# PEER experts in a transformer block: all experts for all tokens, or one indirect gather per chosen slot

## The chip, the cores and the metric

The kernel runs on one core of a Trainium2 chip. The metric is the device time of one execution in microseconds (us); the kernel before was timed three times.

## The reference, cut to what matters

One block of a trunk model for 512 latent tokens of width 2048 (`x1` is the residual after the mixer and the first layer norm). Everything ahead of the PEER layer is left alone by the change except the way its result is handed over. PEER has 8 heads. Each head picks for each token 16 of 16,384 experts, and an expert is one row `u` and one row `v` of 2048 fp32 numbers:

```python
s1, i1 = lax.top_k(s[..., 0, :], PEER_TOPK)
s2, i2 = lax.top_k(s[..., 1, :], PEER_TOPK)
cand_s = (s1[..., :, None] + s2[..., None, :]).reshape(B_, T, PEER_HEADS, n_cand)
cand_i = (i1[..., :, None] * PEER_N_KEYS + i2[..., None, :]).reshape(B_, T, PEER_HEADS, n_cand)
top_s, pos = lax.top_k(cand_s, PEER_TOPK)
idx = jnp.take_along_axis(cand_i, pos, axis=-1)
gates = jax.nn.softmax(top_s, axis=-1).astype(h.dtype)
...
act = jax.nn.gelu(jnp.einsum('nkd,nd->nk', u[i_blk], h_blk), approximate=False)
return jnp.einsum('nk,nkd->nd', g_blk * act, v[i_blk])
```

So each token has 8 x 16 = 128 chosen pairs of rows. The output is `layer_norm(ALPHA * x1 + gate2 * peer, ln2_g, ln2_b)`.

## The kernel before

The stages run one behind the other; a barrier of all engines stands between two of them. `modulation`, `in_projection`, `rglru` and `rwkv` are not touched. `out_projection` ends in a layer norm with channels on the partitions: its result `x1` goes to DRAM, and `h2` is kept split in two fp32r halves, `h_hi` and `h_lo` ([128, 16, 512], channel tiles by tokens). `queries` projects `h2` and takes the 16 best keys of each half head (`best_key`, `best_val`).

`route` takes the tokens in four tiles of 128. Per tile VectorE (DVE) adds the pairs of scores, finds the 16 best of 256 for 8 heads, looks their key numbers up and makes the softmax. Then it builds one-hot matrices (`hot1`, `hot2`, L1685), GpSimd (POOL) puts the gates on one of them (L1581), TensorE (PE) multiplies them (L1603), and so a dense array of gates, 128 x 128 experts by 512 tokens, comes to DRAM as `gates_scratch` (32 MB).

`experts` then computes every expert for every token, in 16 groups of 8 chunks of 128 experts. A unit is 1 MB of weights: SP loads it (`raw`), ScalarE (ACT) copies it to fp32r (`hi`, L1738), DVE makes the rest (`lo`, L1752), and PE multiplies in three passes (hi x hi, hi x lo, lo x hi; L1798), 48 matmuls of 128x512 per unit. A group has 8 `u` units, whose results go through Gelu and are weighted with the gates (loaded by POOL, L1728), and 8 `v` units, whose results DVE adds to `f` (L1769). There are 256 units, 128 of `u` and 128 of `v`. `final` scales, adds `x1`, takes the second layer norm and stores the output. Two buffers each hold `raw`, `hi` and `lo`.

Of the kernel before, what the change touches and what calls it, by code (L numbers as in the profile page):

```python
# [163 lines left out]

# [156 lines left out]

# [143 lines left out]

# [145 lines left out]

# [3 lines left out]

# [54 lines left out]

# [367 lines left out]

# [97 lines left out]

# [48 lines left out]

# [86 lines left out]

# [117 lines left out]

def out_projection(nc, e, a):

    with ExitStack() as ctx:
# [14 lines left out]

        def finish(ctx, sb, normed):
            h2 = [sb(f"h2{b}", [P, LAT]) for b in range(2)]  # L1440
            modded, hi_done, lo_done, stored = sems(nc, ctx, "h2_modded", "h2_hi_done", "h2_lo_done", "x1_stored")

            def on_dve(dve, k):

                dve.wait_ge(normed, k + 1)
                nc.vector.tensor_scalar(h2[k % 2][:], z[:, k, :], e.one_plus_scale2[:, k:k + 1], e.mod[:, 3 * KT + k, 0:1], ALU.mult, ALU.add
                                        ).then_inc(modded, 1)
                dve.wait_ge(hi_done, k + 1)
                nc.vector.tensor_tensor(e.h_lo[:, k, :], h2[k % 2][:], e.h_hi[:, k, :].bitcast(FP32), ALU.subtract).then_inc(lo_done, 1)

            def on_act(act):
                for k in range(KT):
                    act.wait_ge(modded, k + 1)
                    nc.scalar.activation(e.h_hi[:, k, :], h2[k % 2][:], ACT.Copy).then_inc(hi_done, 1)

            def on_sp(sp):
                for q in range(4):
                    sp.wait_ge(normed, 4 * q + 4)
                    sp.dma_start(e.x1_dram[:, 4 * q:4 * q + 4, :], z[:, 4 * q:4 * q + 4, :]).then_inc(stored, 16)
                sp.wait_ge(stored, 64)  # L1460

            return on_act, on_dve, on_sp
# [9 lines left out]

# [15 lines left out]

# [42 lines left out]

R_STEPS = 16
SPREAD = 4
DEPTH = 4
BANKFUL = 4

def route(nc, e, a):

    with ExitStack() as ctx:
        sb = lambda n, s, d=FP32: ctx.enter_context(nc.sbuf_tensor("rt_" + n, s, d))
# [16 lines left out]
        tiles, turns, fills = LAT // P, P // SPREAD, P // BANKFUL
        per_turn = SPREAD // BANKFUL  # L1560
        with nc.Block() as block:
            @block.sync
            def _(sp):
                for dst, src in ((ident, a["ident"]), (iota, a["iota"])):
                    sp.dma_start(dst[:], src).then_inc(const_loaded, 16)
                sp.sem_inc(dense_free, 1)

                with sp.Fori(0, tiles) as t:
                    sp.wait_ge(bank_read, (t + 1) * fills + 4)
                    sp.dma_start(e.gates_dram[:, :, bass.ds(t * P, P)], dense[:]).then_inc(stored, 16)  # L1570
                    sp.wait_ge(stored, 16 * t + 16)
                    sp.sem_inc(dense_free, 1)
# [12 lines left out]
            def _(pe):
                pe.sem_inc(hot_used, DEPTH * per_turn)
                pe.sem_inc(turned, 1)
                pe.wait_ge(const_loaded, 32)
                with pe.Fori(0, tiles) as t:
                    pe.wait_ge(chosen_ready, t + 2)  # L1590
                    pe.wait_ge(sel_ready, t + 1)
                    for j in range(3):
                        last = nc.tensor.transpose(t_acc[:, j * P:(j + 1) * P], chosen[:, j, :], ident[:])
                    last.then_inc(turned, 1)
                    with pe.Fori(0, turns // DEPTH) as i:
                        for b in range(DEPTH):
                            turn = t * turns + DEPTH * i + b
                            pe.wait_ge(gated_ready, turn + 1)
                            for n in range(SPREAD):
                                f = n // BANKFUL  # L1600
                                if n % BANKFUL == 0:
                                    pe.wait_ge(bank_read, turn * per_turn + f + 1)
                                ins = nc.tensor.matmul(g_acc[(b * per_turn + f) % 4][:, (n % BANKFUL) * NK:(n % BANKFUL + 1) * NK],  # L1603
                                                       hot1[b][:, n, :], gated[b][:, n, :], start=True, stop=True)
                                if n % BANKFUL == BANKFUL - 1:
                                    ins.then_inc(hot_used, 1)

            @block.scalar
            def _(act):
                act.sem_inc(sel_ready, 1)  # L1610
                act.sem_inc(bank_read, 4)
                with act.Fori(0, tiles) as t:
                    act.wait_ge(shifted, t + 1)
                    nc.scalar.activation(chosen[:, 2, :], top[:].rearrange("p h k -> p (h k)"), ACT.Exp).then_inc(exp_done, 1)
# [384 lines left out]
```

## Time and profile before

| | us |
|---|---|
| three runs, median (lowest to highest) | 6884.99 (6883.69 to 6888.27) |
| the profiled execution, first to last instruction (its span) | 6879.0 |
| the profiled execution's own time | the record holds its span alone; the median of the runs lies 6.0 above the span |
| PE busy in the span | 6061.1 (88%) |
| DVE busy | 2778.5 (40%) |
| ACT busy | 1685.7 (25%) |
| POOL busy | 366.5 (5%) |
| moved by DMA, all told | 595.47 MB, mean 87 GB/s |

A busy engine is one that executes an instruction; several can be busy at once, so the shares don't add up to one. The PE clock column of a window is the granted clock as a share of 2.4 GHz: 1.00 is 2.4 GHz and 0.50 is 1.2 GHz. The DMA share is the mean busy share of the core's 16 DMA engines.

### The profile page before, as it was taken

How to read it: one execution, taken by the hardware profiler on the slowest of the kernel's cores; microseconds unless marked ns; L12 is line 12 of the kernel's file. 1: busy time of each engine (PE TensorE's matmuls, PEld its weight loads, DVE VectorE, ACT ScalarE, POOL GpSimd, SP SyncE). 2: the span in 40 equal slices, each digit the busy share in tenths (PEclk: the TensorE clock that was granted, in tenths of full speed). 3: DMA queues.
4: the chain of work that ended last, by engine and by line, in shares of the span. 5: the costliest groups of instructions: out<-in, count | busy, mean ns of one | idle time of the engine just before them, and what ended most of it. 6: DMA issues, size and time to landing. Idle time of an engine off the chain costs nothing. (4 is left out here: it accounts for less than half of the span.)

```text
span 6879.0 us, 80488 instructions
## 1 busy us (share of the span) xinstructions
PE 6061.1 (88%) x32312; PEld 4951.1 (72%) x32312; DVE 2778.5 (40%) x3717; ACT 1685.7 (25%) x1951; POOL 366.5 (5%) x426
## 2 busy tenths in 40 slices
PE   6798988699999999959664569999999999999997
PEld 1687855687788877837453458888888888888885
DVE  1333433443433444232579933333333333333333
ACT  0111225333332333222213312222222222222222
POOL 0000010000000000010003400000000000000000
PEclk8899999788887888769887789999999999999998
DMA  5222275100000000031204353333333333333332
GB/s 227 91 86 82 102 250 182 41 21 11 11 8 8 21 11 11 1 109 61 98 31 79 67 144 110 110 106 107 110 110 110 105 108 108 110 110 106 107 108 86
DMA packets 199453, 595.47 MB, mean 87 GB/s; under 512 B 16884, under 2 KB 121972, under 8 KB 146292
## 3 DMA queue, kind: packets, MB, share of 16 engines
q1 hardware_dynamic: 176160, 477.24, 21.2%
q0 software_dynamic: 22976, 115.63, 5.0%
q8 instruction: 135, 2.21, 0.1%
q14 instruction: 34, 0.28, 0.0%
q10 hardware_dynamic: 148, 0.10, 0.0%
HBM read 531.84 MB, written 61.09 MB: 86 GB/s over the span
## 5 line engine op out<-in xcount | busy, mean ns | idle before, releaser
L1798 PE MATMUL ex_u<-h_hi,ex_hi 128*128 128x512 f32 x2048 | 797.6, 389 | 52.5 <-DVE ex_lo L1752 52.5
L1798 PE MATMUL ex_u<-h_lo,ex_hi 128*128 128x512 f32 x2048 | 797.4, 389 | 0.0
L1798 PE MATMUL ex_u<-h_hi,ex_lo 128*128 128x512 f32 x2048 | 797.3, 389 | 0.0
L1798 PE MATMUL ex_v<-ex_w_hi,ex_hi 128*128 128x512 f32 x2048 | 796.7, 389 | 0.0
L1798 PE MATMUL ex_v<-ex_w_lo,ex_hi 128*128 128x512 f32 x2048 | 796.7, 389 | 0.0
L1798 PE MATMUL ex_v<-ex_w_hi,ex_lo 128*128 128x512 f32 x2048 | 796.7, 389 | 0.0
L1738 ACT ACTIVATE ex_hi<-ex_raw 128x2048 fp32r<-128x2048 f32 x256 | 490.3, 1915 | 1100.8 <-PE ex_v L1798 1100.3
L1752 DVE TENSOR_TENSOR ex_lo<-ex_raw,ex_hi 128x2048 fp32r<-128x2048 f32 x256 | 586.5, 2291 | 84.1 <-ACT ex_hi L1738 84.1
L1769 DVE TENSOR_TENSOR f<-f,ex_v 128x512 f32<-128x512 f32 x256 | 164.5, 684 | 843.1 <-PE ex_v L1798 843.1
L1798 PEld LDWEIGHTS ex_u<-h_hi,ex_hi 128*128 128x128 f32 x2048 | 384.9, 188 | 132.7 <-DVE ex_lo L1752 52.7
L1759 DVE TENSOR_TENSOR ex_w<-ex_act,ex_gates 128x512 f32<-128x512 f32 x128 | 88.7, 693 | 882.2 <-ACT ex_act L1743 882.2
L1798 PEld LDWEIGHTS ex_u<-h_hi,ex_lo 128*128 128x128 f32 x2048 | 384.8, 188 | 80.0
L1798 PEld LDWEIGHTS ex_u<-h_lo,ex_hi 128*128 128x128 f32 x2048 | 384.8, 188 | 79.8
L1798 PEld LDWEIGHTS ex_v<-ex_w_hi,ex_lo 128*128 128x128 f32 x2048 | 384.4, 188 | 79.9
L1798 PEld LDWEIGHTS ex_v<-ex_w_lo,ex_hi 128*128 128x128 f32 x2048 | 384.4, 188 | 79.8
L1798 PEld LDWEIGHTS ex_v<-ex_w_hi,ex_hi 128*128 128x128 f32 x2048 | 384.4, 188 | 79.7
L1743 ACT ACTIVATE ex_act<-ex_u 128x512 f32<-128x512 f32 x128 | 76.8, 600 | 1077.3 <-PE ex_u L1798 1077.3
L994 DVE TENSOR_TENSOR rw_X<-rw_bank,rw_level_mask 128x512 f32<-128x512 f32 x240 | 164.4, 691 | 398.3 <-PE rw_bank L1110 396.9
L250 PE MATMUL pb_acc<-x_hi,pb_hi 128*128 128x512 f32 x832 | 213.0, 338 | 72.8 <-DVE pb_lo L221 72.8
L1685 DVE TENSOR_TENSOR rt_hot<-rt_iota,rt_sel 128x512 f32<-128x512 f32 x256 | 259.1, 1088 | 7.8 <-ACT rt_sel L1617 7.8
L1603 PE MATMUL rt_g<-rt_gated,rt_hot 128*128 128x128 f32 x1024 | 186.1, 339 | 86.2 <-POOL rt_gated L1581 85.2
L605 PE MATMUL late_acc<-lru_late_w,cond_act 128*1 128x128 f32 x2048 | 229.2, 275 | 28.1 <-DMA lru_late_w<-in_ada_late 28.1
(349 smaller groups left out, 9245.2 us busy)
## 6 DMA issues: line engine op xcount, KB each, us to landing
ex_raw<-in_peer_u SPq DMA_DIRECT2D x128, 1024.0 KB, 4.8
ex_raw<-in_peer_v SPq DMA_DIRECT2D x128, 1024.0 KB, 4.8
lru_late_w<-in_ada_late POOLq DMA_DIRECT2D x64, 1024.0 KB, 5.1
ada_w<-in_ada_w SPq DMA_DIRECT2D x8, 4096.0 KB, 20.8
gates_scratch<-rt_dense SPq DMA_DIRECT2D x4, 8192.0 KB, 38.9
ex_gates<-gates_scratch POOLq DMA_DIRECT2D x128, 256.0 KB, 3.0
pb_raw<-in_w_in SPq DMA_DIRECT2D x26, 1024.0 KB, 4.8
pl_raw<-in_w_in SPq DMA_DIRECT2D x18, 1024.0 KB, 4.8
```

Source lines behind the costliest of these rows:

```text
L250: last = nc.tensor.matmul(acc[b][s][:], wt[b][:, ks], x[:, k, c0:c0 + w], start=(k == 0 and n == 0), stop=(k == KT - 1 and n == 2))
L605: last = nc.tensor.matmul(late_acc[rows % 2][part:part + 1, col:col + P], e.cond_act[:, k, 0:1], late_w[n % LATE_BUFS][:, k * P:(k + 1) * ...
L994: nc.vector.tensor_tensor((X if level > 1 else T)[:, 4 * q:4 * q + 4, :], take(("X", level, q))[:].rearrange("p (h n) -> p h n", h=4), mas ...
L1603: ins = nc.tensor.matmul(g_acc[(b * per_turn + f) % 4][:, (n % BANKFUL) * NK:(n % BANKFUL + 1) * NK], hot1[b][:, n, :], gated[b][:, n, :], ...
L1685: ins = nc.vector.tensor_tensor(dst[:], iota[:, None, :].to_broadcast(full), sel[:, m, at, None].to_broadcast(full), ALU.is_equal)
L1738: nc.scalar.activation(hi[u % 2][:], raw[u % 2][:], ACT.Copy).then_inc(hi_done, 1)
L1743: nc.scalar.activation(act_[c % 2][:], u_acc[c % 2][:], ACT.Gelu).then_inc(gelu_done, 1)
L1752: nc.vector.tensor_tensor(lo[u % 2][:], raw[u % 2][:], hi[u % 2][:].bitcast(FP32), ALU.subtract).then_inc(lo_done, 1)
L1759: nc.vector.tensor_tensor(w[c % 2][:], act_[c % 2][:], gates[c % 2][:], ALU.mult).then_inc(weighted, 1)
L1769: nc.vector.tensor_tensor(t, t, v_acc[v % 2][h][:], ALU.add).then_inc(added, 1)
L1798: ins = nc.tensor.matmul(out, wt, x, start=first and n == 0, stop=last and n == 2)
```

## The change

`route`, the old `experts` and `final` go. The host lays `u` and `v` side by side, so that `peer_uv` has 16,384 rows of 16 KB. `out_projection` keeps `h2` in fp32, and a new stage, `token_major`, transposes `x1` and `h2` with 128 PE transposes so that tokens lie on the partitions; `x1` goes to DRAM in that layout.

The new `experts` takes the four token tiles and, in each, 128 slots (8 heads x 16). A slot is one indirect gather by POOL: for each of 128 tokens the row of its expert, 128 x 16 KB = 2 MB, into one of five buffers `uv`. DVE makes the dot product of the `u` half with `h2` (`dot`, written over the `u` half), ACT the Gelu of one column, DVE a diagonal matrix of gelu times gate (`weigh`), and PE four fp32 matmuls of 128x512 that add diagonal times `v` into four PSUM banks of `f_acc`. The choice of experts (`route`) is now cut in ten parts. The first tile's are all made ahead of the slots; those of the next tile stand between slots 6, 14, ... 78 of the tile before. `finish` (the residual and the second layer norm, token-major) of a tile stands at slots 3 and 4 of the next one.

```diff
-        e.gates_dram = nc.dram_tensor("gates_scratch", [NK, NK, LAT], FP32, kind="Internal").ap()
+        token_major(nc, e, a, z, h2)
...
+        fills = [(src, q, t) for src in range(2) for q in range(4) for t in range(TOK_TILES)]
...
+                sp.wait_ge(act_taken, 2 * TOK_TILES)
+                sp.wait_ge(dve_taken, 2 * TOK_TILES)
+                sp.dma_start(e.x1_dram.rearrange("t p d -> p t d"), x1_tok[:]).then_inc(stored, 16)
+                sp.wait_ge(stored, 16)
...
+                    for j in range(4):
+                        ins = nc.tensor.transpose(banks[n % 8][:, j * P:(j + 1) * P],
+                                                  (x1, h2)[src][:, 4 * q + j, t * P:(t + 1) * P], ident[:])
...
+                        nc.scalar.activation(dst[src][:, t, q * BANK:(q + 1) * BANK], banks[n % 8][:], ACT.Copy).then_inc(act_taken, 1)
...
+                        nc.vector.tensor_copy(dst[src][:, t, q * BANK:(q + 1) * BANK], banks[n % 8][:]).then_inc(dve_taken, 1)
...
+ROUTE_PARTS = 10
+ROUTE_AT = 6
+ROUTE_EVERY = 8
+FINAL_AT = 3
+SLOTS = PEER_HEADS * TOPK
+BUFS = 5
+DIAGS = 4
...
+            def _(pool):
+                for n in range(total_slots):
+                    t, s = n // SLOTS, n % SLOTS
+                    if s == 0:
+                        pool.wait_ge(chosen_ready, t + 1)
+                    if n >= BUFS:
+                        pool.wait_ge(slot_used, n - BUFS + 1)
+                    pool.indirect_dma_start(uv[n % BUFS][:], None, a["peer_uv"],
+                                            bass.IndirectOffsetOnAxis(expert[:, t, s:s + 1], 0)).then_inc(uv_loaded[n % BUFS], 16)
...
+                    pe.wait_ge(diag_ready, n + 1)
+                    for c in range(D // BANK):
+                        ins = nc.tensor.matmul(f_acc[t % 2][:, c * BANK:(c + 1) * BANK], diag[n % DIAGS][:],
+                                               uv[n % BUFS][:, D + c * BANK:D + (c + 1) * BANK], start=s == 0, stop=s == SLOTS - 1)
+                    ins.then_inc(slot_used, 1)
...
+                def root(t):
+                    act.wait_ge(var_ready, t + 1)
+                    nc.scalar.activation(rstd[:], mv[:, 1:2], ACT.Ln, bias=eps[:]).then_inc(ln_done, 1)
+                    act.wait_ge(ln_done, t + 1)
+                    nc.scalar.activation(rstd[:], rstd[:], ACT.Exp, scale=-0.5).then_inc(rstd_ready, 1)
...
+                    act.wait_ge(dotted, n + 1)
+                    nc.scalar.activation(gelu[:, t, s:s + 1], dots[:, t, s:s + 1], ACT.Gelu).then_inc(gelu_done, 1)
...
+                def dot(n):
+                    t, s, b = n // SLOTS, n % SLOTS, n % BUFS
+                    dve.wait_ge(uv_loaded[b], 16 * (n // BUFS + 1))
+                    nc.vector.tensor_tensor_reduce(out=uv[b][:, 0:D], in0=uv[b][:, 0:D], in1=e.h2_tok[:, t, :], op0=ALU.mult, op1=ALU.add,
+                                                   scale=1.0, scalar=0.0, accum_out=dots[:, t, s:s + 1]).then_inc(dotted, 1)
+
+                def weigh(n):
+                    t, s = n // SLOTS, n % SLOTS
+                    dve.wait_ge(gelu_done, n + 1)
+                    if n >= DIAGS:
+                        dve.wait_ge(slot_used, n - DIAGS + 1)
+                    nc.vector.tensor_scalar(diag[n % DIAGS][:], ident[:], gelu[:, t, s:s + 1], gate[:, t, s:s + 1], ALU.mult, ALU.mult
+                                            ).then_inc(diag_ready, 1)
...
+                for n in range(total_slots):
+                    t, s = n // SLOTS, n % SLOTS
+                    dot(n)
+                    if n:
+                        weigh(n - 1)
+                    if t and s in (FINAL_AT, FINAL_AT + 1):
+                        finish(t - 1, s - FINAL_AT)
+                    part, off = divmod(s - ROUTE_AT, ROUTE_EVERY)
+                    if t + 1 < TOK_TILES and off == 0 and 0 <= part < ROUTE_PARTS:
+                        route(t + 1, part)
...
+    a["peer_uv"] = np.concatenate([g["peer_u"][0], g["peer_v"][0]], axis=1)
```

What DVE has in a row in the `experts` stage of before, inside a group's `u` units (`ex_w_hi`, `ex_w_lo` are the weighted activations in two halves; line numbers are those of the kernel before):

```order
L1752 TENSOR_TENSOR ex_lo0<-ex_raw0,ex_hi0 128x2048
L1757 REGISTER_ALU
L1759 TENSOR_TENSOR ex_w1<-ex_act1,ex_gates1 128x512
L1760 REGISTER_ALU
L1761 CAST ex_w_hi<-ex_w1 128x512
L1763 TENSOR_TENSOR ex_w_lo<-ex_w1,ex_w_hi 128x512
```

What DVE has there in the changed kernel, around slot 3 of the second tile (line numbers of the changed kernel; the first `ISA` row is the dot product, the second writes its sum out):

```order
L1653 ISA ex_uv1,ex_dots<-ex_uv1,h2_tok 128x2048
L1653 ISA ex_dots 128x1
L1661 TENSOR_SCALAR ex_diag2<-ex_ident,ex_gelu,ex_gate 128x128
L1671 TENSOR_TENSOR ex_z<-ex_f0,ex_rows 128x2048
L1673 SCALAR_TENSOR_TENSOR ex_z<-ex_x1,ex_z 128x2048
L1677 BN_STATS ex_stats<-ex_z 128x6 x4
L1679 BN_AGGR ex_mv<-ex_stats 128x2
L1653 ISA ex_uv2,ex_dots<-ex_uv2,h2_tok 128x2048
L1653 ISA ex_dots 128x1
```

One subtraction of 128x2048 per MB of weights has become one product with a sum per 2 MB gathered, and the diagonal follows it one slot late; pieces of `finish` and `route` stand in the same queue.

What PE has from the end of `route` into `experts` before (`rt_g` is the dense array's bank; the loops' bookkeeping stands between), where each unit is 48 matmuls, 12,288 in all:

```order
L1603 MATMUL rt_g3<-rt_gated3,rt_hot1_3 128x128 x4
L1595 REGISTER_ALU
L1595 COMPARE_AND_BRANCH
L1589 REGISTER_ALU
L1589 COMPARE_AND_BRANCH
L1561 UNCONDITIONAL_BRANCH
L1791 UNCONDITIONAL_BRANCH
L1801 UNCONDITIONAL_BRANCH
L1801 ISA
L1798 MATMUL ex_u0<-h_hi,ex_hi0 128x512
L1798 MATMUL ex_u0<-h_lo,ex_hi0 128x512
L1798 MATMUL ex_u0<-h_hi,ex_lo0 128x512
```

And in the changed kernel, one row per slot, 512 rows:

```order
L1576 MATMUL ex_f0<-ex_uv0,ex_diag0 128x512 x4
L1576 MATMUL ex_f0<-ex_uv1,ex_diag1 128x512 x4
L1576 MATMUL ex_f0<-ex_uv2,ex_diag2 128x512 x4
L1576 MATMUL ex_f0<-ex_uv3,ex_diag3 128x512 x4
L1576 MATMUL ex_f0<-ex_uv4,ex_diag0 128x512 x4
```

The 12,288 fp32r matmuls have become 2,048 fp32 matmuls, each group of four waiting for its diagonal.

## Rows read from the trace of the kernel before

**Rows 1.** Windows by stage: start:end, length, busy (instructions) of each engine, PE clock, DMA share, GB/s.

```profile
0.00:3322.00 3322.00, 2857.27 (x18028) 2310.36 (x18028) 1230.41 (x1508) 890.22 (x1331) 129.99 (x170) 0.85 0.20 70
3322.00:3546.00 224.00, 195.84 (x896) 160.22 (x896) 139.97 (x657) 38.61 (x32) 0.00 (x0) 0.93 0.23 80
3546.00:4003.00 457.00, 189.68 (x1036) 161.49 (x1036) 391.54 (x591) 138.17 (x136) 166.22 (x128) 0.69 0.36 74
4003.00:6804.00 2801.00, 2787.40 (x12288) 2307.57 (x12288) 979.78 (x897) 594.82 (x416) 70.25 (x128) 1.00 0.32 108
6804.00:6879.00 75.00, 30.93 (x64) 11.47 (x64) 36.80 (x66) 23.89 (x36) 0.00 (x0) 0.75 0.30 113
```

**Rows 2.** The page's costliest groups, experts and route stages.

```profile
L1798 PE MATMUL ex_u<-h_hi,ex_hi 128*128 128x512 f32 x2048 | 797.6, 389 | 52.5 <-DVE ex_lo L1752 52.5
L1738 ACT ACTIVATE ex_hi<-ex_raw 128x2048 fp32r<-128x2048 f32 x256 | 490.3, 1915 | 1100.8 <-PE ex_v L1798 1100.3
L1752 DVE TENSOR_TENSOR ex_lo<-ex_raw,ex_hi 128x2048 fp32r<-128x2048 f32 x256 | 586.5, 2291 | 84.1 <-ACT ex_hi L1738 84.1
L1685 DVE TENSOR_TENSOR rt_hot<-rt_iota,rt_sel 128x512 f32<-128x512 f32 x256 | 259.1, 1088 | 7.8 <-ACT rt_sel L1617 7.8
```

**Rows 3.** Groups of instructions by line.

```profile
L900 DVE TENSOR_TENSOR_SCAN rw_cum<-rw_restart,rw_sg 128x1024 f32<-128x1024 f32 x12 | 27.4, 2282 | 2.5 <-ACT rw_sg L825 2.5
L1728 POOL DMA_DIRECT2D ex_gates<-gates_scratch x128 | 70.2, 549 | 2664.7 <-DVE ex_w L1759 2608.3 <-DVEq L1748 43.3 <-issue 13.0
L857 ACT ACTIVATE rw_T<-rw_bank 128x512 f32<-128x512 f32 x240 | 143.3, 597 | 379.8 <-PE rw_bank L1123 379.8
```

**Rows 4.** Timeline of PE, transposes in rwkv.

```profile
1271.04 1.94 PE L1075 MATMUL rw_bank<-rw_ident,rw_Bt 128*128 128x128 f32 x8 [11.90 <-DVEq L942]
```

**Rows 5.** Timeline of the first route tile: start, length, instruction, [idle before it].

```profile
3550.89 2.29 DVE L1648 TENSOR_TENSOR rt_score<-best_val 128x2048 f32 x1 [2.54 <-DMA rt_iota<-in_iota]
3569.89 0.31 ACT L1614 ACTIVATE rt_chosen<-rt_top 128x128 f32<-128x128 f32 x1 [37.59 <-DVE rt_top L1658]
3584.44 0.29 DVE L1672 TENSOR_TENSOR rt_chosen<-rt_chosen,rt_total 128x128 f32<-128x128 f32 x1
```

**Rows 6.** Windows of three stretches with loaded DMA engines (columns as in rows 1).

```profile
14.00:70.00 56.00, 55.94 (x138) 12.33 (x139) 0.33 (x2) 1.76 (x3) 0.00 (x0) 1.00 1.01 434
910.00:920.00 10.00, 7.40 (x66) 5.34 (x63) 9.90 (x11) 0.00 (x0) 1.62 (x3) 0.93 1.03 413
3018.00:3030.00 12.00, 0.00 (x0) 0.00 (x0) 3.70 (x3) 3.82 (x2) 9.87 (x9) 0.50 1.04 387
```

**Rows 7.** DMA issues: out<-in, queue, count, KB each, median us from issue to landing.

```profile
ex_raw<-in_peer_u SPq DMA_DIRECT2D x128, 1024.0 KB, 4.8
gates_scratch<-rt_dense SPq DMA_DIRECT2D x4, 8192.0 KB, 38.9
out_dram<-f SPq DMA_DIRECT2D x4, 1024.0 KB, 4.3
```

**Rows 8.** Timeline of PE's weight loads in the first matmuls on `ada_w`.

```profile
16.57 0.13 PEld L142 LDWEIGHTS ada_acc<-ada_w,cond_act 128*2 128x2 f32 x1 [0.72 <-issue]
17.42 0.13 PEld L142 LDWEIGHTS ada_acc<-ada_w,cond_act 128*2 128x2 f32 x1 [0.72 <-issue]
18.79 0.09 PEld L142 LDWEIGHTS ada_acc<-ada_w,cond_act 128*2 128x2 f32 x1 [0.34 <-issue]
19.22 0.09 PEld L142 LDWEIGHTS ada_acc<-ada_w,cond_act 128*2 128x2 f32 x1 [0.34 <-issue]
```

**Rows 9.** Window of a route stretch (columns as in rows 1).

```profile
3596.00:3656.00 60.00, 40.05 (x232) 34.09 (x230) 58.00 (x58) 30.99 (x30) 36.34 (x28) 0.86 0.00 0
```

**Rows 10.** Groups of DVE instructions in the first route tile.

```profile
L1486 DVE MATCH_REPLACE8 rt_rest<-rt_top,rt_score 128x256 f32<-128x256 f32 x8 | 3.2, 436 | 0.0
L1483 DVE FIND_INDEX8 rt_pos<-rt_top,rt_score 128x8 uint32<-128x256 f32 x8 | 3.2, 427 | 0.0
```

**Rows 11.** Groups of instructions in the last 79 us.

```profile
L1392 ACT ACT_TABLE_LOAD x1 | 1.3, 1283 | 0.0
```

More of the change, by code:

```diff
@@ L1453, in on_act @@
                     act.wait_ge(modded, k + 1)
[L1454 to L1462, printed above, removed]
-        layer_norm(nc, a, "ln1_", z, a["ln1_g"], a["ln1_b"], finish)
+                    nc.scalar.activation(e.h_hi[:, k, :], h2[:, k, :], ACT.Copy).then_inc(hi_done, 1)
@@ L1559, in route @@
[L1559 to L1560 removed]
+        expert_f = sb("expert_f", [P, P])
+        expert, gate = sb("expert", [P, TOK_TILES, SLOTS], U32), sb("gate", [P, TOK_TILES, SLOTS])
+        dots, gelu = sb("dots", [P, TOK_TILES, SLOTS]), sb("gelu", [P, TOK_TILES, SLOTS])
+        uv = [sb(f"uv{b}", [P, 2 * D]) for b in range(BUFS)]
+        diag = [sb(f"diag{b}", [P, P]) for b in range(DIAGS)]
+        rows = sb("rows", [P, 3, D])
@@ L1584, in _ @@
             @block.tensor
             def _(pe):
[L1586 to L1606, printed above, removed]
@@ new lines, in _ @@
+                for part in range(ROUTE_PARTS):
+                    route(0, part)
+                for n in range(total_slots):
+                    t, s = n // SLOTS, n % SLOTS
+                    dot(n)
[6 more added lines that the diff above has]
+                        route(t + 1, part)
@@ new lines, in _, with best_part @@
+                weigh(total_slots - 1)
+                finish(TOK_TILES - 1, 0)
+                finish(TOK_TILES - 1, 1)
+EXP_PART = 4
+def best_part(nc, c, landed, vals, positions, source, other, n, part):
+    at = slice(8, 16) if part == 2 else slice(0, 8)
+    src = other if part == 2 else source
+    if part in (0, 2):
+        nc.vector.tensor_copy(landed[:, 0:1], landed[:, 1:2])
+        for r in range(n):
+            ins = nc.vector.max(vals[:, r, at], src[:, r, :])
+        c.ordered(ins)
+    if part in (1, 2):
+        nc.vector.tensor_copy(landed[:, 0:1], landed[:, 1:2])
+        for r in range(n):
+            ins = nc.vector.max_index(positions[:, r, at], vals[:, r, at], src[:, r, :])
+        if part == 1:
+            for r in range(n):
+                ins = nc.vector.match_replace(other[:, r, :], vals[:, r, at], src[:, r, :], LOWEST)
+        c.ordered(ins)
@@ L1884, in tail @@
             out_projection(nc, e, a)
-            with ExitStack() as picks:
-                e.best_key, e.best_val = (picks.enter_context(nc.sbuf_tensor(n, [P, TOK_TILES, HP, TOPK], FP32))
-                                          for n in ("best_key", "best_val"))
-                queries(nc, e, a)
-                route(nc, e, a)
-            f = inner.enter_context(nc.sbuf_tensor("f", [P, KT, LAT], FP32))
-            experts(nc, e, a, f)
-            final(nc, e, a, f, out)
+            queries(nc, e, a)
+        experts(nc, e, a, out)
 def position_tables():
```

403 lines of the change are left out of this document (153 added, 250 removed).

## Prediction, written before the run

> **What bounds the kernel now.** I read the windows by stage first. The last three stages, which the change replaces, take 3333 us of the 6879: 457 for `route`, 2801 for `experts`, 75 for `final` [rows 1]. In `experts` PE is busy for 2787 of 2801 us at clock 1.00, while the DMA engines are busy for 0.32 of it. So the stage is as long as PE's 12,288 matmuls: 2801 / 12,288 = 0.228 us each. The groups of the page agree: a matmul waits for nothing but the first unit (52.5 us over all groups), and ACT stands idle for 1100 us until PE frees a buffer [rows 2]. In `route` DVE is busy for 392 of 457 us [rows 1]. Everything ahead of 3546 us stays, but for one stage put in.
>
> **The change, part by part.** *Removed:* all that lies behind 3546, 3333 us.
>
> *`token_major`, added ahead of the queries.* 128 transposes of 128x128. The trace has eight such in 1.94 us, with PE just out of an idle stretch of 11.9 us [rows 4], so 0.24 each or 31 us for all; once PE runs at its higher clock, half, 16. ACT and DVE take 16 fills each: at 0.60 us (the eviction of 128x512 in [rows 3]) that is 10 us beside it. The 4 MB store of `x1` starts after half of the fills, 8 to 15 us, and at the best rate below (434 GB/s) moves for 10 us and lands some 2 later. I take 26 us with the barrier, from 20 to 40.
>
> *Head of the stage.* Choosing the first tile's experts is DVE's old chain: from 3546 the first sum starts at 3550.89 and the softmax ends at 3584.7 [rows 5]; two small operations of 0.3 come on top: 39 us, nothing beside it. Then a first gather must land: 1 MB takes 4.8 us from issue to landing [rows 7], of which 1.05 MB / 434 GB/s = 2.4 is moving, so 2.4 is latency; with POOL's issue 3 us beyond the transfer itself.
>
> *The 512 slots.* Four resources serve a slot, and the slowest sets its length.
> - DMA: 128 x 16,384 B = 2.097 MB, 1074 MB for all slots. The stretch 14 to 70 us, where loads of `ada_w` (rows of 32 KB) queue behind each other, shows all 16 engines full (share 1.01) at 434 GB/s; two other full stretches, with shorter rows mixed in, give 413 and 387 [rows 6]. That is 4.83, 5.08 and 5.42 us a slot. Rows of 16 KB lie between, scattered reads may cost something: I take 5.1.
> - PE: four fp32 matmuls of 128x512. Each has two weight loads in the trace, and these follow each other every 0.85 us at first and every 0.43 us afterwards [rows 8]; the clock over the stretch is 1.00 in the mean [rows 6], so these are the two levels, 1.2 and 2.4 GHz. A matmul is then 0.86 us at 2.4 GHz, a slot 3.4; at 1.2 GHz 6.8.
> - DVE: the dot product reads 2 x 2048 numbers as `ex_lo` does, 2.29 us [rows 2], then a sum is written out and a 128x128 diagonal made, 0.15 + 0.3: 2.75. The product with a running sum is not in the trace. The other bound is the scan, which also carries a sum: 1024 elements in 2.28 us [rows 3], so 4.5 for 2048, and 4.95 a slot. I take the former, since a sum over the row needs no result per element. The Trainium skill ("Vector Engine (DVE) Microarchitecture Reference", section 7, Points that are easy to get wrong) says that a scalar-tensor-tensor shape with two sources in SBUF that aren't bf16 halves its throughput, since no port is left to read the accumulator back; by it the slot would be DVE's 4.95 too, and no run here has shown it.
> - POOL: one issue. A plain DMA of 128 rows is 0.55 us [rows 3]; an indirect one reads 128 indices as well. Above I bound it by an operation of DVE that it may have to wait out, 0.55 + 2.29 = 2.8. Both lie under 5.1.
>
> So the slot is the DMA engines' 5.1 us: 512 x 5.1 = 2611 us. That holds while enough gathers are queued. A buffer comes round every 5 x 5.1 = 25.5 us. From landing to `slot_used` it needs the dot (2.3), the next slot's landing and dot (5.1, since `weigh` stands one slot late), 0.3 and PE's 3.4: 11.4 with waits. Issue, latency and its own transfer are 0.6 + 2.4 + 5.1 = 8.1. The remaining 6 us are the slack.
>
> *Stalls.* DVE's long pieces eat into that slack. The longest part of `route` is 8 x (0.427 + 0.436) and small loads, some 8 us [rows 10]; the others are at most two operations of 2.29. `finish` is about 7 us at slot 3, and at slot 4 a wait for ACT with two table loads of 1.28 [rows 11], then 6: 16 together. Per tile (16 - 6) + (8 - 6) = 12 at most, less what DVE regains in the 2.35 us that each slot leaves it; 20 us for three tiles.
>
> *Tail.* Behind the last landing: dot 2.3, Gelu and diagonal 0.6, PE 3.4, `finish` 7 + 3 + 6, and 1 MB out in 4.3 [rows 7], 28 us with waits.
>
> *Sum:* 3546 + 26 + 39 + 3 + 2611 + 20 + 28 = 6273 against the span of 6879. The median of the runs is 6885, 6 above the span, so I say 6279. Slots of 4.83 to 5.42 us make it 6140 to 6440.
>
> 2. *Scattered rows come slower, but above the break-even.* The loads of 1 MB in `experts` show 108 GB/s at share 0.32 [rows 1], 338 GB/s if that share were 1. At 338 to 390 a slot is 5.4 to 6.2 us, 6430 to 6840. 13%, with the case of the rule in it.
> 3. *Slower than before: the gather falls under the break-even.* The stage may cost 3333 - 26 - 39 - 3 - 28 = 3237 us, so 6.32 us a slot, 332 GB/s. The place is the read side, 128 scattered addresses per gather. The price, with 300 GB/s, is 7.0 us a slot and 7250. For it: the only far row of a worse pattern, the 8 MB store of short pieces in 38.9 us [rows 7], runs at 216 GB/s. Against it: its pieces are 512 B, and these are 16 KB. 10%.
> 4. *PE stays at 1.2 GHz,* because it rests between slots: 6.8 us a slot, and then 7150. Against it: at the lower level PE would work without a rest, and in `route` PE at 0.67 busy was granted 0.86 [rows 9], which makes 4.0 us a slot, under 5.1. It decides from a mean clock of 0.67. 4%.
> 5. *POOL's indices cost over 6.3 us.* Nothing in the trace prices that. 3%.
> 6. *Ties* within 0.2%, which is about what a measurement of this kernel can tell from no change: 2%.
>
> **How the numbers follow.** The forecast (DMA-bound, 4.8 to 5.42 us) has 58%; rivals 1 to 6 have 10, 13, 10, 4, 3 and 2. Faster by over 0.2%: 58 + 10 + 13 = 81%; within 0.2%: 2%; slower: 17%. The range reaches from 6120, just under 4.83 us a slot, to 6760, a slot of 6.05, which takes in rival 1 and most of rival 2; about 2 in 10 stay outside, nearly all above.
>
> **What the profile after would show.** Right: DMA share near 1 and 400 to 440 GB/s between about 3620 and 6240; `ex_uv` landing in a steady beat of 5.1; DVE's dot released by the DMA of `ex_uv`; PE idle for a third of the time and released by the diagonal; POOL released by PE's `slot_used`. Wrong in the price of the dot: its row would say 4.4 us in place of 2.3. Wrong in the clock: matmuls of a slot in 6.8 us and the DMA share at 0.75. Wrong in POOL: the issue row long and POOL never idle. Rivals 2 and 3: DMA share near 1, but fewer GB/s. The forecast fails most easily by the rate of scattered rows, since each 0.1 us of a slot is 51 us.

## The result, and the profile after

The changed kernel takes 6201.74 us, the median of 4 runs (6191.05 to 6207.8), against 6886.63 before (4 runs, 6883.69 to 6897.67). The ratio is 0.9001, 95% interval 0.8989 to 0.9014. The profiled execution took 6191.05 us, with a span of 6189.4. Faster was forecast, at 6279 us: 77 above the measurement, inside the range.

The windows by stage, with the columns of [rows 1]: what stays, `token_major`, the queries, the head of the new stage, its slots, its tail.

```profile
0.00:3322.00 3322.00, 2857.73 (x18028) 2311.31 (x18028) 1226.72 (x1503) 888.12 (x1329) 130.62 (x170) 0.85 0.20 69
3322.00:3348.00 26.00, 16.73 (x128) 16.49 (x128) 14.24 (x22) 10.81 (x18) 0.00 (x0) 0.75 0.29 119
3348.00:3572.00 224.00, 196.24 (x896) 160.51 (x896) 136.45 (x634) 38.59 (x32) 0.00 (x0) 0.94 0.24 85
3572.00:3620.00 48.00, 0.00 (x0) 0.00 (x0) 37.31 (x111) 1.59 (x2) 4.30 (x5) 0.50 0.34 118
3620.00:6160.00 2540.00, 1917.79 (x4080) 752.07 (x4080) 1446.38 (x1818) 125.31 (x535) 709.43 (x508) 0.98 1.00 425
6160.00:6189.40 29.40, 7.13 (x16) 2.96 (x16) 14.52 (x14) 3.27 (x5) 0.00 (x0) 0.69 0.08 36
```

Where 3333 us were replaced, 2643 now stand: 26 of `token_major` and 2617 from 3572 on. The resource that is full has changed: in [rows 1] PE was busy all through `experts` and the DMA engines for 0.32; from 3620 to 6160 us it is the DMA engines, share 1.00 at 425 GB/s in the mean, and PE is busy for 0.76. The groups of instructions from 3560 us on say the same by what ended each engine's idle time:

```profile
L1576 PE MATMUL ex_f<-ex_uv,ex_diag 128*128 128x512 f32 x4096 | 1924.9, 615 | 680.0 <-DVE ex_diag L1661 679.6
L1653 DVE CUSTOM_DVE_ANT_0 ex_uv<-ex_uv,h_tok 128x2048 f32<-128x2048 f32 x512 | 1173.5, 2292 | 1098.0 <-DMA ex_uv<-in_peer_uv,ex_expert 1097.3
...
L1565 POOL DMA_INDIRECT ex_uv<-in_peer_uv,ex_expert x512 | 713.7, 1394 | 2384.1 <-PE ex_f L1576 1797.5 <-DVE ex_expert L1647 565.4 <-issue 21.2
L1661 DVE TENSOR_SCALAR ex_diag<-ex_ident,ex_gelu,ex_gate 128x128 f32<-128x128 f32 x512 | 175.9, 343 | 0.0
```

DVE's dot is released by the landing of `ex_uv`, PE by the diagonal, POOL by PE's release of a buffer. So it's a ring, and its slowest part, the transfer, sets the pace. A steady stretch of the timeline (start, length, instruction, idle before it) shows the beat:

```profile
4999.41 2.29 DVE L1653 CUSTOM_DVE_ANT_0 ex_uv<-ex_uv,h_tok 128x2048 f32<-128x2048 f32 x1 [2.30 <-DMA ex_uv<-in_peer_uv,ex_expert]
...
5001.14 1.38 POOL L1565 DMA_INDIRECT ex_uv<-in_peer_uv,ex_expert  x1 [3.49 <-PE ex_f L1576]
...
5001.63 0.34 DVE L1661 TENSOR_SCALAR ex_diag<-ex_ident,ex_gelu,ex_gate 128x128 f32<-128x128 f32 x1
...
5002.03 3.70 PE L1576 MATMUL ex_f<-ex_uv,ex_diag 128*128 128x512 f32 x8 [1.16 <-DVE ex_diag L1661]
...
5004.23 2.29 DVE L1653 CUSTOM_DVE_ANT_0 ex_uv<-ex_uv,h_tok 128x2048 f32<-128x2048 f32 x1 [2.25 <-DMA ex_uv<-in_peer_uv,ex_expert]
...
5009.09 2.29 DVE L1653 CUSTOM_DVE_ANT_0 ex_uv<-ex_uv,h_tok 128x2048 f32<-128x2048 f32 x1 [2.30 <-DMA ex_uv<-in_peer_uv,ex_expert]
```

Dot follows dot by 4.82 and 4.86 us. Quiet windows hold 431 GB/s, and 2.097 MB / 431 GB/s = 4.866. Not all windows are quiet:

```profile
3700.00:3740.00 40.00, 29.31 (x64) 11.20 (x63) 24.65 (x55) 1.42 (x7) 10.31 (x9) 1.00 1.01 432
3740.00:3780.00 40.00, 31.52 (x64) 12.78 (x64) 24.57 (x44) 1.62 (x8) 9.69 (x8) 0.91 0.95 400
3780.00:3820.00 40.00, 30.39 (x63) 12.61 (x64) 23.76 (x37) 4.50 (x11) 10.37 (x8) 0.91 0.95 393
...
4700.00:4740.00 40.00, 30.70 (x68) 12.05 (x67) 21.18 (x25) 1.62 (x8) 10.51 (x8) 1.00 1.01 431
```

In the 80 us behind a part of `route` that holds DVE until 3739.6 (3740 to 3820, with the next part in it), the rate is 400 and 393 GB/s, and PE's granted clock 0.91. The chain of waits (start, length, what) tells how the one leads to the other:

```profile
3717.82 12.84 DMA ex_uv<-in_peer_uv,ex_expert
...
3733.30 3.15 DVE ex_pos L1721 x8
3736.45 0.84 DVE ex_rest L1724 x3
...
3739.64 0.04 DVE ex_uv L1653
...
3742.25 16.74 PE ex_f L1576 x32
...
3759.25 13.62 DMA ex_uv<-in_peer_uv,ex_expert
```

A transfer lands (3730.65), the next one's dot stands behind 6.3 us of `max_index` and `match_replace`, PE is done with its slot at 3736.99 and rests for 5.26 us, and then works off the matmuls of four slots in 16.74 us, 4.2 a slot where the steady beat above has 3.70. For these 17 us the chain runs through PE and not through a transfer: gathers are issued late, and the DMA share of the window is 0.95.

### The profile page after: what moved, and what is told of

It reads as the page before. It is cut to its first block and busy times, and to the rows that moved or that the text cites. A ratio compares the mean times of both kernels' runs of the same rounds, so it can differ in the third digit from the quotient of the medians.

```text
span 6189.4 us, 58049 instructions
## 1 busy us (share of the span) xinstructions
PE 4995.6 (81%) x23148; PEld 3243.3 (52%) x23148; DVE 2875.6 (46%) x4099; ACT 1067.7 (17%) x1921; POOL 844.3 (14%) x682
## 5 line engine op out<-in xcount | busy, mean ns | idle before, releaser
L1576 PE MATMUL ex_f<-ex_uv,ex_diag 128*128 128x512 f32 x4096 | 1924.9, 615 | 680.0 <-DVE ex_diag L1661 679.6
L1576 PEld LDWEIGHTS ex_f<-ex_uv,ex_diag 128*128 128x128 f32 x4096 | 755.0, 193 | 1849.3 <-DVE ex_diag L1661 1066.1
L1653 DVE CUSTOM_DVE_ANT_0 ex_uv<-ex_uv,h_tok 128x2048 f32<-128x2048 f32 x512 | 1173.5, 2292 | 1098.0 <-DMA ex_uv<-in_peer_uv,ex_expert 1097.3
L1565 POOL DMA_INDIRECT ex_uv<-in_peer_uv,ex_expert x512 | 713.7, 1394 | 2384.1 <-PE ex_f L1576 1797.5
L1058 PE MATMUL rw_bank<-rw_Tt,rw_X 128*128 128x128 f32 x1920 | 253.6, 275 | 0.0
L1058 PE MATMUL rw_bank<-rw_X,rw_Tt 128*128 128x128 f32 x1920 | 253.6, 275 | 0.0
L1045 PEld LDWEIGHTS rw_bank<-rw_T,rw_Mb 128*128 128x128 f32 x1920 | 240.0, 206 | 12.9 <-issue 11.6
L1045 PE MATMUL rw_bank<-rw_T,rw_Mb 128*128 128x128 f32 x1920 | 245.9, 290 | 0.0
L1058 PEld LDWEIGHTS rw_bank<-rw_Tt,rw_X 128*128 128x128 f32 x1920 | 233.7, 192 | 0.0
L1058 PEld LDWEIGHTS rw_bank<-rw_X,rw_Tt 128*128 128x128 f32 x1920 | 233.7, 192 | 0.0
L186 DVE TENSOR_TENSOR pb_lo<-pb_raw,pb_hi 128x2048 fp32r<-128x2048 f32 x26 | 59.6, 2292 | 259.8 <-ACT pb_hi L162 259.8
```

The costliest lines, as they stand in the source:

```text
L186: nc.vector.tensor_tensor(lo[b][:], raw[b][:], hi[b][:].bitcast(FP32), ALU.subtract).then_inc(lo_done, 1)
L1045: ins = nc.tensor.matmul(out[:, j * C:(j + 1) * C], Mb[:, sl, 0, :], ident[:] if level == 1 else T[:, sl, :], start=True, stop=True)
L1058: ins = nc.tensor.matmul(out[:, j * C:(j + 1) * C], first[:, sl, :], second[:, sl, :], start=True, stop=True)
L1565: pool.indirect_dma_start(uv[n % BUFS][:], None, a["peer_uv"], bass.IndirectOffsetOnAxis(expert[:, t, s:s + 1], 0)).then_inc(uv_loaded[n % ...
L1576: ins = nc.tensor.matmul(f_acc[t % 2][:, c * BANK:(c + 1) * BANK], diag[n % DIAGS][:], uv[n % BUFS][:, D + c * BANK:D + (c + 1) * BANK], s ...
L1653: nc.vector.tensor_tensor_reduce(out=uv[b][:, 0:D], in0=uv[b][:, 0:D], in1=e.h2_tok[:, t, :], op0=ALU.mult, op1=ALU.add, scale=1.0, scalar ...
```

## The experiments

**Is it the bytes?** Two kernels. In the first each gathered row is 8 KB, `u` alone, which PE also takes in place of `v` (so `v` is left out, and DVE writes its products to a buffer of their own):

```diff
-        uv = [sb(f"uv{b}", [P, 2 * D]) for b in range(BUFS)]
+        uv = [sb(f"uv{b}", [P, D]) for b in range(BUFS)]
...
-    a["peer_uv"] = np.concatenate([g["peer_u"][0], g["peer_v"][0]], axis=1)
+    a["peer_uv"] = np.ascontiguousarray(g["peer_u"][0])
```

> The gathered rows are 8 KB: the host leaves v out, and PE multiplies the diagonal with the u half in its place (the output is not PEER's). The number of gathers (512), of rows in each (128), and all work of POOL, DVE, ACT and PE per slot stay. Theory bytes: the slot of 4.86 us in the changed kernel is 2.1 MB at 431 GB/s; with 1.05 MB the transfer is 2.4 us and PE's four fp32 matmuls, 3.43 us, become the bound: 3.5 us a slot, 512 x (4.95 - 3.5) = 740 us less, near 5450 us. Rival per row: if the slot is set by what each index or descriptor costs, nothing changes: near 6190 us.

Measured: 5564.52 us (one run). In the second the row numbers are a fixed table in rising order in place of the chosen experts:

```diff
-                                            bass.IndirectOffsetOnAxis(expert[:, t, s:s + 1], 0)).then_inc(uv_loaded[n % BUFS], 16)
+                                            bass.IndirectOffsetOnAxis(row_ids[:, s:s + 1], 0)).then_inc(uv_loaded[n % BUFS], 16)
```

> The gather's indices come from a table, 128 s + p, so that the 128 rows of a gather lie one behind the other in DRAM; all else is as in the changed kernel, the choice of experts too, only that its result isn't used for the gather (so the output is not PEER's). Theory bytes: scattered rows of 16 KB cost nothing, 6190 us within 15. Rival: scattering costs something; then the beat of 4.86 us falls towards 4.7 us, the best 10 us of plain loads in the trace (446 GB/s), and the time to about 6110 us.

Measured: 6198.81 us (one run). Windows of each, two with half rows first:

```profile
3700.00:3740.00 40.00, 34.86 (x75) 14.52 (x74) 31.72 (x81) 1.82 (x9) 15.10 (x11) 0.91 0.66 239
...
4140.00:4180.00 40.00, 39.09 (x90) 16.55 (x89) 31.87 (x43) 2.23 (x11) 17.01 (x12) 1.00 0.82 300
```
```profile
4700.00:4740.00 40.00, 30.71 (x68) 11.95 (x67) 21.30 (x25) 1.62 (x8) 10.57 (x8) 1.00 1.00 430
```

With half the bytes the engines are at 0.82 in the second window and PE, busy for 39.09 of 40 us, is the bound: the span shrinks by 627 us and stops at the next resource. The 740 us expected are missed by 113. The expectation had left no stalls in: by the starts of the dots, slots 10 to 85 of the first three tiles, with choosing between them, take 3.81 to 3.87 us in place of 3.5 (76 us in all; the first window is one of these, at clock 0.91 and 239 GB/s), and the first ten slots of the other three, with LayerNorm, 4.39 to 4.72 (32 us). The slots with nothing beside them take 3.53 to 3.63. Rows in order run at 430 GB/s, as scattered ones do, and the time is that of the changed kernel. Scattering rows of 16 KB over the table costs nothing that shows here; rivals 2 and 3 fall.

**What does the slack hold up?** Fewer buffers for gathered rows, one constant changed: `BUFS = 4`, then `BUFS = 3`.

> Four gather buffers in place of five. Account of the buffer's round, by the trace of the changed kernel: landing to slot_used is one beat and 6.5 us (dot 2.4, diagonal 0.4, PE 3.5, waits), issue to landing at least 8.0 us; so 4 beats must hold 1 beat + 14.5 us, a beat of at least 4.83 us: just enough, but without slack. Theory: the beat of 4.86 us stays where DVE only has slots, and every piece of route and finish delays the gathers by its full length: 3 x (33 + 13) = 140 us of stalls in place of 49, near 6280 us. Rival, buffers play no part: 6190 us.

> Three gather buffers. By the same account 3 beats = 1 beat + 14.5 us: 7.25 us a slot, 512 x (7.25 - 4.95) = 1180 us more and about 90 of stalls: near 7460 us, slower than the kernel before. PE then rests for 3.8 us a slot; if it is granted the lower clock for that, its four matmuls take 6.9 us, a beat is 8.95 us, and the time near 8240 us. Rival, the buffers are not what limits: below 6400 us.

A sixth buffer wasn't tried. Measured: 6680.33 and 8036.91 us (one run each). Four buffers cost 479 us, where the slack account had given some 80, and three come out between its two values, 7460 and 8240. With three, the ring lies open, since little queues. Its chain of waits:

```profile
5693.03 8.23 DMA ex_uv<-in_peer_uv,ex_expert
...
5703.90 5.95 PE ex_f L1576 x8
...
5710.11 8.40 DMA ex_uv<-in_peer_uv,ex_expert
```

From the issue of a gather to its landing it takes 8.23 to 8.40 us: the 8.1 of the account. But a slot on PE takes 5.9, not 3.4. The timeline of the kernel with four buffers shows why, at a landing that came late:

```profile
4706.39 3.70 PE L1576 MATMUL ex_f<-ex_uv,ex_diag 128*128 128x512 f32 x8 [1.93 <-DVE ex_diag L1661]
4706.92 0.19 PEld L1576 LDWEIGHTS ex_f<-ex_uv,ex_diag 128*128 128x128 f32 x1 [0.24 <-issue]
...
4710.80 2.29 DVE L1653 CUSTOM_DVE_ANT_0 ex_uv<-ex_uv,h_tok 128x2048 f32<-128x2048 f32 x1 [4.47 <-DMA ex_uv<-in_peer_uv,ex_expert]
...
4713.41 0.50 PEld L1576 LDWEIGHTS ex_f<-ex_uv,ex_diag 128*128 128x128 f32 x2 [4.16 <-DVE ex_diag L1661]
4713.42 8.93 PE L1576 MATMUL ex_f<-ex_uv,ex_diag 128*128 128x512 f32 x16 [3.33 <-DVE ex_diag L1661]
4714.43 0.34 PEld L1576 LDWEIGHTS ex_f<-ex_uv,ex_diag 128*128 128x128 f32 x1 [0.52 <-issue]
...
4716.14 0.34 PEld L1576 LDWEIGHTS ex_f<-ex_uv,ex_diag 128*128 128x128 f32 x1 [0.52 <-issue]
4716.75 0.19 PEld L1576 LDWEIGHTS ex_f<-ex_uv,ex_diag 128*128 128x128 f32 x1 [0.27 <-issue]
```

At 4706.92 PE's weight loads take 0.19 and follow 0.24 behind one another, a step of 0.43, the higher of the two levels of [rows 8]. Then its matmuls rest for 3.33 us (the weight loads for 4.16), and until 4716.14 the loads take 0.34 with 0.52 between them, a step of 0.86: the lower one. So a late landing doesn't cost its own lateness alone: PE then holds its buffer longer (5.95 against 3.70 us in the chain with three buffers), the next gather is issued later, and PE rests again. From the first dot to the last the granted clock fell with the buffers, 0.98, 0.89, 0.75, and of the steps between a slot's weight loads 3, 17 and 38% are at the lower level.

The clock isn't all that the slack account lacked, though. With four buffers another stretch of the chain has PE at 3.7 us a slot, and the transfers are long:

```profile
5965.54 11.59 DMA ex_uv<-in_peer_uv,ex_expert
...
5979.77 3.72 PE ex_f L1576 x8
...
5983.74 10.36 DMA ex_uv<-in_peer_uv,ex_expert
...
5996.74 3.71 PE ex_f L1576 x8
```

Taken over the quiet slots of all tiles (90 and up) the beat with four buffers is 5.86 us, so three beats are 17.6 where the account had 14.5. Most of these 3.1 us lie between the release of a buffer and the dot on its next rows, 10.8 us in the mean where the account had 8.0. PE has the smaller part, some 0.4 (4.16 us a slot, 3.73 in the changed kernel). So gathers still queue behind one another at times, though the mean rate over the slots is only 358 GB/s. That a slower slot on PE bunches them is likely, but no run here separates the two.

**Can the slack be had back without a buffer?** The diagonal of a slot is made right behind its own dot:

```diff
                     dot(n)
-                    if n:
-                        weigh(n - 1)
+                    weigh(n)
```

> One edit to the changed kernel: slot n's diagonal is made right behind slot n's dot (VectorE waits for its GELU), instead of behind dot n+1. From landing to the release of the buffer it is then dot 2.4 + GELU 0.4 + diagonal 0.4 + four matmuls 3.5 = 6.7 us, where it was 11.4, so the slack of a buffer's round goes from some 5 us to some 9.5. Theory A (stalls are slack overrun by VectorE's long pieces, with PE's lower clock behind them): the 49 us fall to 10 to 20, 6160 to 6175 us. Theory B (they are not a matter of slack, or VectorE's wait for the GELU costs it as much as it gives): 6195 to 6210 us. The steady beat of 4.86 us stays by both.

> The diagonal right behind the dot, as in the run before, and four buffers for gathered rows instead of five. With four buffers and the diagonal one slot late the run took 6680 us. The account of a buffer's round says: four beats are 19.4 us, less 6.7 from landing to release, less 8.1 from release to the next landing, leaves 4.6 us, as much as five buffers leave in the changed kernel; by theory A (the slack is what counts, and losing it starts the fall of PE's clock) it takes 6190 to 6240 us. By theory B (four buffers are too few transfers in flight for the DMA queues to keep their rate, whatever VectorE's order is) it stays at 6500 to 6700 us.

Measured: 6171.94 us (5 runs, 6163.48 to 6176.78) with five buffers, and 6213.93 (2 runs) with four. The second decides: the same four buffers that took 6680 us take 466 less, by the order of two instructions of DVE. So four buffers are enough for the engines (422 GB/s from the first dot to the last); it was the slack that lacked. From the first dot to the last it is 2514.4 us with five buffers, so 29 us of stalls are left where 10 to 20 were expected, though the time is inside its range. Ratios to the kernel before are 0.8954 (0.8941 to 0.8966) and 0.9019 (0.9000 to 0.9037).

**Where do the stalls come from?** From the first to the last dot the changed kernel takes 2535.8 us, and 511 beats of 4.863 are 2485: 51 us too many. One kernel leaves out choosing for tiles 1 to 3, the next also puts all LayerNorms behind the last product:

```diff
-                    if t + 1 < TOK_TILES and off == 0 and 0 <= part < ROUTE_PARTS:
-                        route(t + 1, part)
...
-                    if t and s in (FINAL_AT, FINAL_AT + 1):
-                        finish(t - 1, s - FINAL_AT)
```

> Leaves out the choosing of experts for token tiles 1 to 3: they gather tile 0's expert numbers again, and take its gates. The ten pieces of choosing between the dots of tiles 0 to 2 are gone; the gathers, dots, diagonals and products are as in the changed kernel. Theory A (the 49 us by which the first to the last landing exceeds 511 beats of 4.86 us are transfers that start late, because a piece of choosing or of the LayerNorm holds up a dot and then PE runs on at its lower clock): about 35 to 40 us are given back, the LayerNorm pieces of tiles 1 to 3 keep the rest: 6150 to 6170 us, and 40-us windows without a LayerNorm piece all at 428 to 434 GB/s. Theory B (the dips are the DMA engines' or the memory's own, whatever VectorE does): 6190 to 6205 us, dips in the same number.

> As the run without choosing for tiles 1 to 3, and the LayerNorm of all four tiles with its loads of x1 and stores of the result is moved behind the last product (so tiles 0 and 1 are normed from the sums of tiles 2 and 3: a part of the result is left out). Between first and last dot nothing is left but the slots. The accounts differ on the first-to-last dot, which is 2535.8 us in the changed kernel and 2515.2 without choosing, where 511 beats of 4.863 us make 2485. Theory A (14.6 us of the rest are the 6.29 MB of x1 and result at 431 GB/s on the same engines, 9 to 12 are gathers that start late behind the LayerNorm's pieces): 2486 to 2493 us. Theory C (the rest is in the gathers themselves, a beat that is slower now and then for the memory's own reasons): 2505 to 2515 us. The whole run takes about what the run without choosing takes, 6175 to 6195 us, since three LayerNorms of 16 us and their loads come behind the end.

Measured: 6180.66 us (4 runs, 6171.74 to 6185.95) and 6208.01 (2 runs; in it each of the three moved LayerNorms stands alone behind the end, 88.7 us behind the last dot's start, more than was expected). The dots of the changed kernel, of the first and of the second (count, ns min/median/max, first and last start):

```profile
L1653 DVE CUSTOM_DVE_ANT_0 ex_uv<-ex_uv,h_tok x512: 2228/2293/2294, 3622.6 to 6158.4; 128x2048 f32<-128x2048 f32 x171
```
```profile
L1651 DVE CUSTOM_DVE_ANT_0 ex_uv<-ex_uv,h_tok x512: 2227/2292/2295, 3632.5 to 6147.7; 128x2048 f32<-128x2048 f32 x171
```
```profile
L1648 DVE CUSTOM_DVE_ANT_0 ex_uv<-ex_uv,h_tok x512: 2291/2292/2295, 3619.7 to 6117.0; 128x2048 f32<-128x2048 f32 x171
```

In the trace of the changed kernel there is one queue beside the gathers' own that moves data in the slots (packets, MB, share of 16 engines):

```profile
q0 software_dynamic: 73646, 1072.43, 99.2%
q1 hardware_dynamic: 864, 6.29, 0.6%
```

First to last dot they take 2535.8, 2515.2 and 2497.3 us, one trace each. A second trace of the changed kernel has 2539.6 (3630.6 to 6170.2), so some 4 us in such a difference mean nothing. Choosing then costs 20.6, the LayerNorms 17.9, and 12.3 stay with nothing beside the slots. Of the LayerNorms' 17.9 the transfers of `x1` and of the result would explain 14.6: the 6.29 MB of the second row at 431 GB/s, on engines that are full. That is an estimate; no run moved these transfers alone. The expectation had put 35 to 40 us to choosing, and missed; the last kernel came out between its two theories (2486 to 2493, and 2505 to 2515). With the diagonal behind its dot the same count is 2514.4: that edit alone gives back as much as choosing cost, though choosing is all there.

The 12.3 aren't spread evenly. In the kernel with nothing beside the slots the beat is 4.854 in the median, 2480.4 for 511 of them, and of the 16.9 us above that fourteen long beats carry 14.1: one of 6.21 us (slot 12), and from slot 98 on thirteen of 5.81 to 5.85, each 32 slots behind the last. One of them:

```profile
4249.15 2.29 DVE L1648 CUSTOM_DVE_ANT_0 ex_uv<-ex_uv,h_tok 128x2048 f32<-128x2048 f32 x1 [2.29 <-DMA ex_uv<-in_peer_uv,ex_expert]
...
4254.99 2.29 DVE L1648 CUSTOM_DVE_ANT_0 ex_uv<-ex_uv,h_tok 128x2048 f32<-128x2048 f32 x1 [3.28 <-DMA ex_uv<-in_peer_uv,ex_expert]
```

In the trace's DMA packets each of the thirteen has one of 8 KB on an instruction queue (q14) about 2 us ahead of its dot. Twelve more such packets pass with no beat that long, so it stays open whether they are the cause.

**A better version.** Diagonal behind the dot, choosing in 14 finer parts, and tile 0's heads 0 and 1 chosen first, so that the gathers start before the others are chosen; then the same once more, on another chip (its label names an edit that it does not have), and with the LayerNorm in six pieces; and the changed kernel again beside them.

```diff
-ROUTE_PARTS = 10
+ROUTE_PARTS = 14
+ROUNDS = ((0, 0, 2), (0, 2, 8), (1, 0, 8), (2, 0, 8), (3, 0, 8))
...
-                    if s == 0:
-                        pool.wait_ge(chosen_ready, t + 1)
+                    if n == 0:
+                        pool.wait_ge(chosen_ready, 1)
+                    if n == 32:
+                        pool.wait_ge(chosen_ready, 2)
```

> Three edits to the changed kernel. The diagonal right behind the dot; choosing cut into 14 pieces of at most 3.5 us instead of ten of up to 10.5; and for tile 0 the experts of heads 0 and 1 are chosen first, on a quarter of the work, so that the gathers start before heads 2 to 7 are chosen, between the first dots. The head of 48 us before the first dot should fall by 25 to 30 us, and the stalls of 49 us to 10 or less: 6125 to 6150 us if both are right; if the stalls aren't a matter of slack but the head is, 6165 to 6180 us; if choosing between the first dots starves PE as much as it saves, 6190 us or above.

> The kernel of the early start once more, unchanged, for one look on the chip on which the next is timed: 6143 to 6162 us, 2519 us from the first dot to the last.

> The kernel of the early start, with the LayerNorm between dots cut into six pieces of at most 2.8 us (one behind each of slots 3 to 8) instead of two of 7.3 and 5.9 us. Theory A (a gather starts late when a piece overruns the round's slack): the windows at 412, 400 and 395 GB/s rise to 420 or more, and 6 to 10 us are given back, 6140 to 6150 us. Theory B (they come of the 1 MB loads and stores alone, which stay): 6148 to 6158 us, windows as before.

> The changed kernel itself, again, on the same chip as the two before: 6191 to 6208 us, so that the versions are set against it and not against another chip's.

Measured: 6153.29 us (5 runs, 6143.56 to 6161.58; ratio to before 0.8934, 0.8922 to 0.8947); 6155.83 (one run); 6154.49 (5 runs, 6146.38 to 6156.59); the changed kernel 6202.82 (5 runs, 6197.41 to 6208.36). On one chip, with the six pieces, that is 48 us less than the changed kernel, 0.8%, and none of the runs overlap. From the first operation of choosing to the first dot it is 23.9 us where the changed kernel has 42.8 (3585.56 to 3609.5, and 3587.80 to 3630.6), 19 and not the 25 to 30 expected. The stalls did not fall to 10 us or less either: first to last dot it is 2516.7 to 2519.4 us, no less than with the diagonal alone, so the finer parts of choosing gave nothing, and 6153.29 lies just above the 6125 to 6150 expected. The six pieces of LayerNorm left the total as it was, 2516.6 us. From 4240 to 4320 the rate rose, 432 and 428 GB/s where two pieces have 424 and 418, and the first ten slots of tiles 1 to 3 take 5.23 us and not 5.44 to 5.49; but the next 75 take 0.03 us more each. What LayerNorm still costs isn't the length of its pieces.

## Why the prediction was right, and where its numbers were not

The bound, the ring and who releases whom came as written, and the beat is as steady, though at 4.86 and not 5.1. The times of the profiled execution, against 6273 forecast, less 6189.4 measured, 83.6 us over:

| term | forecast | measured | from |
|---|---|---|---|
| up to the end of the queries | 3572 | 3572 | windows by stage |
| to the first dot | 47.1 (39 + 3 + 5.1) | 50.6 | choosing starts at 3580.03, dot at 3622.6 |
| 511 more slots | 2606 | 2485 | beat 4.863 |
| stalls | 20 | 51 | 2535.8 - 2485 |
| from the last dot's start | 28 | 31.0 | 6158.4 to 6189.4 |

(The stalls' 51 hold the 12 that stay with nothing beside the slots.) The one step that carried the miss is the size of the slot: "Rows of 16 KB lie between, scattered reads may cost something: I take 5.1." The allowance was not needed; the best stretch of [rows 6], 434 GB/s, was the row to take, 4.83 for 4.86. It made the sum 121 us too long.

The rule weighed there, about 358 GB/s a core for transfers from HBM (the Trainium skill, "DMA: Bandwidth & Descriptors", Where 436 GB/s comes from), is not borne out here: 431 GB/s stood through whole windows with the other cores at rest. Its 6670 us didn't come, and rivals 2 and 3 fell with it.

The stalls were put too low by 31 us. LayerNorm's own transfers, 14.6 us by their bytes, weren't in the sum at all, and the 12.3 that stay without any piece weren't either: 27 of the 31. DVE's pieces, the only stalls in the sum, had 20 and come to about 24, but the other way round: it gave a tile (16 - 6) for LayerNorm and (8 - 6) for choosing, and measured are 20.6 us for choosing and some 3 for what LayerNorm does beside its transfers. So the 20 was close by luck. It weighed each piece alone against the slack, and PE's fall to the lower level after a rest was kept to a rival of its own (the fourth), as something that lasts or doesn't, when it comes in spells that eat the slack. Of the slack's terms, landing to release was right (11.4 for 11.2 in the median), and so was issue to landing where nothing queues (8.1 for 8.0 to 8.4).

The other prices: the dot is 2292 ns, as taken, and 83 ns more for writing its sum out; rival 1 falls, and with it, for this instruction, the rule of the Trainium skill ("Vector Engine (DVE) Microarchitecture Reference", section 7, Points that are easy to get wrong), which would have halved its rate: 2048 elements in 2292 ns, 0.89 a ns, is what the subtraction of [rows 2] has. The `SCALAR_TENSOR_TENSOR` of `finish` (L1673, two fp32 sources in SBUF, no sum written out) takes 2292 ns too. The diagonal is 0.34. PE's slot is 3.70 at clock 1.00, 0.3 over the 3.4 taken, and PE, busy for 0.76 of the slots' time, was granted 0.98 over it, so rival 4 falls. POOL's issue is 1.39 us in the mean, inside 0.55 to 2.8; rival 5 falls. `token_major` is 26 us, as summed.

## What to carry to other kernels

Where one transfer queue is full, its beat is the price and all else is slack: sum landing to release and release to landing, and compare with buffers times beat. Shorten the way from landing to release before buying a buffer; here two swapped instructions of VectorE did what a fifth buffer did. And leave slack beyond the sum: with four buffers the account came out at a beat of 4.83 us and the run at 5.9, since one late landing may put PE on the lower clock level just when time is short, and gathers that bunch land later than one alone. Count every small transfer that shares the full engines by its bytes.

## What the runs showed of the hardware

An indirect DMA's issue on POOL takes 0.93 to 0.94 us by itself. If it starts while DVE runs an operation with both its sources in SBUF, it takes what is left of that operation and 0.81 us more (and never under 0.93); beside an operation with one source, or with one of two in PSUM (`ex_f`), it takes 0.94 all the same. Three pairs from the run with four buffers:

```profile
4806.39 2.28 DVE L1638 TENSOR_REDUCE ex_chosen<-ex_score 128x128 f32<-128x2048 f32 x1
...
4806.89 0.94 POOL L1565 DMA_INDIRECT ex_uv<-in_peer_uv,ex_expert  x1 [7.59 <-PE ex_f L1576]
...
5161.07 2.28 DVE L1671 TENSOR_TENSOR ex_z<-ex_f,ex_rows 128x2048 f32<-128x2048 f32 x1
...
5161.27 0.94 POOL L1565 DMA_INDIRECT ex_uv<-in_peer_uv,ex_expert  x1 [2.50 <-PE ex_f L1576]
...
5513.71 2.28 DVE L1633 TENSOR_TENSOR ex_score<-ex_iota,ex_k_f 128x2048 f32<-128x2048 f32 x1
...
5514.16 2.65 POOL L1565 DMA_INDIRECT ex_uv<-in_peer_uv,ex_expert  x1 [7.80 <-PE ex_f L1576]
```

In the changed kernel 451 of the 512 issues start beside a dot, whose sources are both in SBUF, and 447 of these take the dot's rest and 0.81 us, give or take 0.04. Where the two start together the issue goes free: with half rows and with four buffers the 20 issues that start up to 0.041 us behind a dot's start all take 0.94, those from 0.046 on take 3.06. With the diagonal behind the dot, which moves the issues out of the dots' way, 257 do, and the mean falls from 1394 ns to 1051:

```profile
L1565 POOL DMA_INDIRECT ex_uv<-in_peer_uv,ex_expert x512 | 538.1, 1051 | 2529.5 <-PE ex_f L1576 1946.8 <-DVE ex_expert L1647 561.2 <-issue 21.6
```

This is read from overlaps in the traces; no run was made for it.
